# A fused two-block network on one core: modulation loads issued three or four weight blocks behind the place that frees their slots

## The chip, the core and the metric

One core of a Trainium2 chip runs the whole kernel. The time is the device time of one execution in microseconds (us); for the kernel before, three timed runs are given by their median. The profile is one more execution, recorded by the hardware profiler. The engines are TensorE (PE), VectorE (DVE), ScalarE (ACT), GpSimd (POOL) and SyncE (SP), whose queue issues the large DMA loads here.

## The reference, cut to what matters

Two blocks of two layers each work on 256 tokens `x` and 256 context tokens, 1024 wide, in float32. Every layer has six modulation vectors of 1024, computed from a condition vector by a 1024 x 6144 matrix. They scale, shift and gate the normalised tokens around a mixer and a gated feed-forward network of width 2816:

```python
mod = (c_act @ w_mod[l] + b_mod[l])[:, None, :]
modc = cc_act @ w_mod[l] + b_mod[l]
sh1, sc1, g1, sh2, sc2, g2 = jnp.split(mod, 6, axis=-1)
...
x = x + g1 * (y_x @ w_out[l])
x = x + g2 * swiglu(rmsnorm(x, norm2_g[l]) * (1.0 + sc2) + sh2, w_gu[l], w_down[l])
...
def swiglu(h, w_gu, w_down):
    gate, up = jnp.split(h @ w_gu, 2, axis=-1)
    return (jax.nn.silu(gate) * up) @ w_down
```

The second block has the same frame with attention as its mixer and its own matrices `mod_w_2`, `ffn_w_in_2` and `ffn_w_out_2` (in the profile `mod_w`, `ffn_w_in`, `ffn_w_out`). The first two layers are the kernel's layers 0 and 1, the others 2 and 3.

## The kernel before, in words

**Weight blocks.** All large matrices are cut into 210 blocks of 1 MB or less (`Plan.item`, numbered 0 to 209 in the order of use). SP loads them one after another into a ring of four slots (`weight_slots`). The load of block g waits until block g - 4 has been split (`weights`, line 607). Splitting makes two float32r parts of a float32 block: ScalarE writes `weights_high`, and VectorE `weights_low`, the rest. PE multiplies high by high, high by low and low by high, and `weights_high` and `weights_low` hold two blocks each.

**Quarter stages.** In layers 0 and 2 most of the feed-forward's first product runs "by quarters": a block's product is built of seven smaller ones (P1 to P7, each 12 matmuls) on sums of weight quarters and of token halves. GpSimd makes the weight sums (L683 to L691), ScalarE (L2654) and VectorE (L1952) split quarters six steps (`LOOK`) ahead of their multiplication, and VectorE adds the products up (L1982, L1990, L1998). Two blocks, the gate's and the value's side, make a pair. A first run takes pairs 2 to 5 (blocks 20 to 27 in layer 0, 122 to 129 in layer 2), a second run, behind the first half of the down projection, pairs 6 to 10 (blocks 36 to 45 in layer 0). The seven quarters of a block come in the order P7, P6, (P2 of the next block), P5, (P1 of the next block), P3, P4.

**Modulation.** The modulation matrices are used in thirds of a layer's 2048 columns. Eight of the twelve thirds are multiplied on PE, in eight steps each: step s takes 128 rows, a load of 1 MB into one of two `modulation_slots` (slot s % 2, `SIDES` = 2), and eight matmuls. The 64 steps have places in PE's program (`places` in `Plan.schedule`). In the first run of a quarter stage two stand at `("quarters", L)`, behind the first two quarters, and two each at `("hidden", L, 5)`, `("hidden", L, 7)` and `("hidden", L, 9)`, behind the last quarter of pairs 2, 3 and 4. In the second run of layer 0 two each stand behind pairs 7, 8, 9 and 10. Each place is written with a block number g in `places`: the block behind which it stands, for "quarters" the first of the run. The four other thirds are summed on VectorE from small row blocks in the down projections ("blocks" and "conditions" in the load list).

**Order on SP.** SP's program is one list: for each weight block g first the loads that `load_before[g]` names, then block g. A step's load waits, on SP, until PE has multiplied the step that had its slot (`stepped`, two steps earlier). While SP waits, everything behind it in the list waits too. Lines 218 to 225 choose the block before which a step's load stands: six blocks behind the place of step s - 2.

The lines that the change touches are in `Plan.schedule`; the step that uses the result is the loop at the end of `sync_program`. Order is all that follows from `load_before`; the waits of the other engines name events, not positions.

Of the kernel before, what the change touches and what calls it, by code (L numbers as in the profile page):

```python
# [88 lines left out]
SIDES = 2  # L89
# [44 lines left out]
class Plan:  # L134
# [54 lines left out]
    def schedule(self):  # L189

        self.mod_steps, self.mod_turn, self.mod_end = {}, {}, {}
        self.load_before = {}
        places = [(("start", k), -1) for k in range(KD)]
        places += [(("proj", 0, e), self.proj[0][e // 2]) for e in (5, 5, 7, 7, 9, 9, 11, 11)]
        places += [(("mlstm", 0, e), self.proj[0][-1]) for e in range(1, 9)]
        for L, first in ((0, (4, 14)), (2, (4,))):
            if L == 2:
                places += [(("mlstm", 1, e), self.proj[1][-1]) for e in range(1, 9)]
                places += [(("proj", 2, e), self.proj[2][e // 2]) for e in (5, 5, 7, 7, 9, 9, 11, 11)]
            for f0 in first:  # L200
                places += [(("quarters", L), self.gu[L, 2][0])] * 2 if f0 == 4 else []
                places += [(("hidden", L, f | 1), self.gu[L, f // 2][1]) for f in range(f0, f0 + (6 if f0 == 4 else KD))]
        assert len(places) == KD * len(STEPPED)
        self.block_at, u = {}, 0
        for L in FAST:
            for part in range(2):
                for f, n in enumerate(BLOCKS_OF_TILE):
                    self.block_at["down", L, part, f] = range(u, u + n)
                    u += n
        assert u == 16 * len(SUMMED)  # L210
        self.block_of_item = {b: self.down[place[1], place[2]][place[3]] for place, bs in self.block_at.items() for b in bs}
        self.block_after = {0: 4, 16: 5, 32: 8}
        self.step_after = {KD * 4: 15, KD * 5: 31}
        for s, (place, g) in enumerate(places):
            self.mod_steps.setdefault(place, []).append(s)
            if s % KD == KD - 1:
                self.mod_end[place] = s // KD
        for s in range(KD, len(places)):
            n = s - s % KD
            if n in self.step_after and s - n < SIDES:  # L220
                before = self.block_of_item[self.step_after[n]] + 4
            else:
                g = places[s - SIDES][1]
                before = g + 6 if g >= 0 else 3
            self.load_before.setdefault(before, []).append(("step", s))
        for u in range(16 * len(SUMMED)):
            at = u - u % 16
            if at in self.block_after and u - at < 3:
                before = places[KD * self.block_after[at] - 1][1] + 4
                if u == at:  # L230
                    self.load_before.setdefault(before, []).append(("conditions", u // 16))
            else:
                before = self.block_of_item[u - 3] + 4
            self.load_before.setdefault(before, []).append(("block", u))
        self.mod_turn = {("proj", 0, 13): 1, ("mlstm", 0, 9): 2, ("down", 0, 0, 1): 3, ("down", 0, 1, 1): 6, ("mlstm", 1, 9): 7,
                         ("out", 2, 0): 8, ("down", 2, 0, 1): 9}
# [2869 lines left out]
```

## Time and profile before

| | us |
|---|---|
| median of three timed runs | 2156.19 |
| the three runs | 2155.13 to 2156.57 |
| profiled execution | 2149.87 |
| its span, first to last instruction | 2148.4 |
| PE busy | 2033.5 (95%) |
| VectorE busy | 1387.4 (65%) |
| ScalarE busy | 1013.7 (47%) |

Times in the rows are counted from the span's start. In a timeline each row has the start, the time from there to the end of the last of its instructions, the engine, line and operation, and in brackets the idle time before it and what ended that. DMA rows on SP (printed SPq) are issues, not transfers. The first quarter stage of layer 0 lies between 340 and 440 us, its second run between 520 and 637, and the one of layer 2 between 1370 and 1467.

### The profile page before, as it was taken

The numbers are of one execution on the slowest core, as the hardware profiler recorded it, in microseconds if no ns is written. First come the engines' busy times: TensorE is split into PE (matmuls) and PEld (weight loads), VectorE is DVE, ScalarE is ACT, GpSimd is POOL, SyncE is SP. The second block draws the span as 40 slices with busy tenths as digits, with TensorE's granted clock in tenths as the row PEclk, the third lists the DMA queues.
The fourth block names the chain that finished last, engine by engine and source line by source line (L and its number), as shares of the span: only waits on it lengthen the run. The fifth ranks groups of instructions, "written<-read, shape, count | busy, mean of one in ns | idle before, by whom it ended". The sixth has DMA issues, their size and how long they took to land.

```text
span 2148.4 us, 32247 instructions
## 1 busy us (share of the span) xinstructions
PE 2033.5 (95%) x12804; PEld 1683.5 (78%) x12804; DVE 1387.4 (65%) x2299; ACT 1013.7 (47%) x1810; POOL 422.6 (20%) x308
## 2 busy tenths in 40 slices
PE   6999999999999899999999899999999999989999
PEld 4776677888987786999966337788898766769999
DVE  4394657867978666655554434786798865566555
ACT  3444644432543646544553343454255256555443
POOL 1000316512531004100100241552154100000000
PEclk9999999999999999999999999999999999999999
DMA  9641521548448535456535002144832731114564
GB/s 340 210 156 60 177 79 59 187 130 277 139 161 290 177 98 202 148 165 212 158 113 184 18 1 79 59 157 153 274 104 85 225 113 63 59 40 158 164 210 118
DMA packets 276742, 311.62 MB, mean 145 GB/s; under 512 B 6128, under 2 KB 260208, under 8 KB 269424
## 3 DMA queue, kind: packets, MB, share of 16 engines
q1 hardware_dynamic: 271888, 304.90, 43.3%
q10 hardware_dynamic: 4704, 4.65, 0.7%
q8 instruction: 102, 1.67, 0.3%
q14 instruction: 48, 0.39, 0.1%
HBM read 308.48 MB, written 1.05 MB: 144 GB/s over the span
## 4 chain that ended last, share of the span: by engine, by line
PE 69%; DVE 15%; ACT 7%; POOL 3%; DMA 3%; issue 3%; ACTq 0%; SPq 0%; DVEq 0%; POOLq 0%
PE bank L779 68%; DVE weights_low L1571 3%; ACT weights_high L2376 2%; DVE weights_low L1952 2%; DVE scratch L1563 1%; DVE yT L1563 1%; DMA modulation_slots<-p_modulation_rows 1%; DVE input_low L1563 1%; DVE modulation_slots L1597 1%; DMA parameter_columns<-p_columns 1%; PE bank L788 1%; DVE xT L1563 1%; DVE hidden_low L1966 1%; DVE big L2095 1%; DMA modulation_slots<-w_mod 0%
## 5 line engine op out<-in xcount | busy, mean ns | idle before, releaser
L779 PE MATMUL bank<-input_high,weights_high 128*128 128x256 f32 (+1 forms) x2336 | 750.7, 323 | 27.5 <-DVE scratch L1990 10.2
L779 PE MATMUL bank<-input_high,weights_low 128*128 128x256 f32 (+1 forms) x2336 | 736.8, 317 | 0.0
L779 PE MATMUL bank<-input_low,weights_high 128*128 128x256 f32 (+1 forms) x2336 | 715.9, 318 | 5.3 <-DVE input_low L1563 5.2
L779 PEld LDWEIGHTS bank<-input_high,weights_high 128*128 128x128 f32 x2336 | 441.4, 189 | 87.4 <-issue 29.4
L1571 DVE TENSOR_TENSOR weights_low<-weight_slots,weights_high 128x1024 fp32r<-128x1024 f32 (+2 forms) x344 | 386.0, 1161 | 185.3 <-ACT weights_high L2376 185.0
L779 PEld LDWEIGHTS bank<-input_low,weights_high 128*128 128x128 f32 x2336 | 435.1, 189 | 43.2 <-DVE input_low L1563 9.7
L779 PEld LDWEIGHTS bank<-input_high,weights_low 128*128 128x128 f32 x2336 | 441.2, 189 | 33.5
L2376 ACT ACTIVATE weights_high<-weight_slots 128x1024 fp32r<-128x1024 f32 (+2 forms) x348 | 314.4, 950 | 149.5 <-PE bank L779 136.4
L1952 DVE TENSOR_TENSOR weights_low<-weight_slots,weights_high 128x512 fp32r<-128x512 f32 x216 | 233.5, 1100 | 35.3 <-ACT weights_high L2654 33.2
L779 PE MATMUL bank<-hidden_high,weights_high 128*128 128x256 f32 (+1 forms) x704 | 238.5, 339 | 0.6 <-DVE weights_low L1571 0.4
L779 PE MATMUL bank<-hidden_low,weights_high 128*128 128x256 f32 (+1 forms) x704 | 237.4, 337 | 0.0
L779 PE MATMUL bank<-hidden_high,weights_low 128*128 128x256 f32 (+1 forms) x704 | 237.3, 337 | 0.0
L750 POOL TENSOR_TENSOR yT<-yT 128x256 f32<-128x256 f32 (+1 forms) x66 | 67.5, 1027 | 642.7 <-ACT yT L2402 514.4
L2654 ACT ACTIVATE weights_high<-weight_slots 128x512 fp32r<-128x512 f32 x216 | 129.2, 622 | 38.0 <-POOL weight_slots L688 19.7
L779 PEld LDWEIGHTS bank<-hidden_high,weights_high 128*128 128x128 f32 x704 | 132.1, 188 | 18.8 <-issue 2.3
L779 PEld LDWEIGHTS bank<-hidden_high,weights_low 128*128 128x128 f32 x704 | 132.1, 188 | 16.2
L779 PEld LDWEIGHTS bank<-hidden_low,weights_high 128*128 128x128 f32 x704 | 132.2, 188 | 15.7
L1563 DVE SCALAR_TENSOR_TENSOR xT<-bank,modulation,xT 128x256 f32<-128x256 f32 x144 | 64.5, 480 | 123.9 <-PE bank L779 123.1
L779 PE MATMUL bank<-token_sums,weights_high 128*128 128x256 f32 x576 | 105.6, 282 | 4.1 <-ACT scratch L2701 2.6
L683 POOL TENSOR_TENSOR weight_sum<-weight_slots 128x512 f32<-128x512 f32 x36 | 50.5, 1402 | 290.7 <-DVE weights_low L1952 148.5
L2402 ACT ACTIVATE yT<-xT 128x256 f32<-128x256 f32 (+1 forms) x64 | 32.9, 522 | 138.5 <-DVE xT L1563 133.1
L779 PEld LDWEIGHTS bank<-token_sums,weights_high 128*128 128x128 f32 x576 | 88.2, 189 | 5.7 <-ACT scratch L2701 3.4
(284 smaller groups left out, 2773.8 us busy)
## 6 DMA issues: line engine op xcount, KB each, us to landing
weight_slots<-w_gu SPq DMA_DIRECT2D x44, 1024.0 KB, 5.2
weight_slots<-ffn_w_in SPq DMA_DIRECT2D x44, 1024.0 KB, 5.2
modulation_slots<-p_modulation_rows SPq DMA_DIRECT2D x64, 512.0 KB, 4.9
modulation_slots<-mod_w SPq DMA_DIRECT2D x32, 1024.0 KB, 6.6
modulation_slots<-w_mod SPq DMA_DIRECT2D x28, 1024.0 KB, 6.6
weight_slots<-w_in SPq DMA_DIRECT2D x24, 1024.0 KB, 8.1
weight_slots<-w_down SPq DMA_DIRECT2D x16, 768.0 KB, 5.1
weight_slots<-ffn_w_out SPq DMA_DIRECT2D x16, 768.0 KB, 5.1
```

The lines of the kernel that those rows point to most:

```text
L683: pool.tensor_tensor(m.weight_sum[:, :, :], a21, a22, ALU.add).then_inc(m.weights_added.sem, 1)
L750: pool.tensor_tensor(o, yT[:, 2 + q, t] if k == 1 else o, yT[:, 2 + i % 4, t], ALU.add).then_inc(m.square_joined.sem, 1)
L779: return pe.matmul(o, w, r, start=start, stop=stop, skip_group_check=shared)
L788: return pe.transpose(o, a, ident[0:a.shape[0], 0:a.shape[0]])
L1563: return stt(out=o, in0=a, scalar=s, in1=b, op0=op0, op1=op1)
L1571: tt(m.w_low[:, g % 2, c], m.ring[:, g % SLOTS, c], m.w_high[:, g % 2, c].bitcast(F32), ALU.subtract).then_inc(m.low_made.sem, 1)
L1597: stt(out=m.block_slot(u), in0=m.block_slot(u), scalar=1.0, in1=m.condition_row(), op0=ALU.mult, op1=ALU.mult, accum_out=m.mods[:, l4, 0, ...
L1952: tt(low, m.raw(run, j), high.bitcast(F32), ALU.subtract).then_inc(m.low_made.sem, 1)
L1966: tt(m.a_low[:, local, :], m.prod[:, f % 2, :], m.a_high[:, local, :].bitcast(F32), ALU.subtract).then_inc(m.hid_low.sem, 1)
L2376: F(m.w_high[:, g % 2, c], m.ring[:, g % SLOTS, c], ACT.Copy).then_inc(m.high_made.sem, 1)
L2402: F(yT[:, 2 + k % 4, t], xT[:, k, t], ACT.Square).then_inc(m.squared.sem, 1)
L2654: F(m.split(j)[0], m.raw(run, j), ACT.Copy).then_inc(m.high_made.sem, 1)
```

## The change

A step's load is still issued some weight blocks behind the place of step s - 2, but the number depends on the kind of that place: four blocks where it is a "hidden" place, three where it is the "quarters" place, six everywhere else as before.

```diff
             if n in self.step_after and s - n < SIDES:
                 before = self.block_of_item[self.step_after[n]] + 4
             else:
-                g = places[s - SIDES][1]
-                before = g + 6 if g >= 0 else 3
+                place, g = places[s - SIDES]
+                before = g + {"hidden": 4, "quarters": 3}.get(place[0], 6) if g >= 0 else 3
             self.load_before.setdefault(before, []).append(("step", s))
```

Eighteen steps move. The engines' own programs are the same; only SP's list is in another order.

| steps | multiplied at | load before block, before | after |
|---|---|---|---|
| 26, 27 | hidden 5, layer 0 | 26 | 23 |
| 28, 29 | hidden 7 | 27 | 25 |
| 30, 31 | hidden 9 | 29 | 27 |
| 34, 35 | hidden 17 | 45 | 43 |
| 36, 37 | hidden 19 | 47 | 45 |
| 38, 39 | hidden 21 | 49 | 47 |
| 58, 59 | hidden 5, layer 2 | 128 | 125 |
| 60, 61 | hidden 7 | 129 | 127 |
| 62, 63 | hidden 9 | 131 | 129 |

(Steps 32 and 33, the first of a third that waits for summed blocks, keep their place, as do those of the projections.)

SP's list in the first run of layer 0's quarter stage, before. The `w_mod` rows are loads of modulation steps (24 and 25 are the last two of the eight ahead), the `w_gu` rows weight blocks 17 to 25, 26 and 27, and `w_down` block 28:

```order
L595 DMA modulation_slots<-w_mod 128x2048 x8
L611 DMA weight_slots<-w_gu 128x8x256 x9
L595 DMA modulation_slots<-w_mod 128x2048 x2
L611 DMA weight_slots<-w_gu 128x8x256
L595 DMA modulation_slots<-w_mod 128x2048 x2
L611 DMA weight_slots<-w_gu 128x8x256
L611 DMA weight_slots<-w_down 128x12x128
L595 DMA modulation_slots<-w_mod 128x2048 x2
L604 DMA modulation_slots<-p_condition_rows 128x1024
```

The same stretch of SP's list after:

```order
L595 DMA modulation_slots<-w_mod 128x2048 x8
L611 DMA weight_slots<-w_gu 128x8x256 x6
L595 DMA modulation_slots<-w_mod 128x2048 x2
L611 DMA weight_slots<-w_gu 128x8x256 x2
L595 DMA modulation_slots<-w_mod 128x2048 x2
L611 DMA weight_slots<-w_gu 128x8x256 x2
L595 DMA modulation_slots<-w_mod 128x2048 x2
L611 DMA weight_slots<-w_gu 128x8x256
L611 DMA weight_slots<-w_down 128x12x128
L604 DMA modulation_slots<-p_condition_rows 128x1024
```

Steps 26 and 27 now stand ahead of blocks 23, 24 and 25, steps 28 and 29 ahead of blocks 25 and 26, and steps 30 and 31 ahead of block 27. Layer 2 has the same pattern.

SP's list in the second run of layer 0, as a difference; the first row is the load of steps 32 and 33, the `w_gu` rows are blocks 38 to 45 of the run, and the other `mod_w` rows are later steps:

```order
 L595 DMA modulation_slots<-mod_w 128x2048 x2
-L611 DMA weight_slots<-w_gu 128x8x256 x7
+L611 DMA weight_slots<-w_gu 128x8x256 x5
+L595 DMA modulation_slots<-mod_w 128x2048 x2
+L611 DMA weight_slots<-w_gu 128x8x256 x2
 L595 DMA modulation_slots<-mod_w 128x2048 x2
 L611 DMA weight_slots<-w_gu 128x8x256
```

Steps 34 and 35 now stand ahead of blocks 43 and 44, and steps 36 and 37 ahead of block 45.

## Rows read from the trace of the kernel before

**Rows 1.** The page, part 1: busy time, share of the span and instructions of each engine.

```profile
PE 2033.5 (95%) x12804; PEld 1683.5 (78%) x12804; DVE 1387.4 (65%) x2299; ACT 1013.7 (47%) x1810; POOL 422.6 (20%) x308
```

**Rows 2.** Waits of PE over the span: engine, line, waited for, total us, times, longest us.

```profile
PE bank L779 <- DMA modulation_slots<-w_mod: 15.2, 4, 6.7
...
PE bank L779 <- DMA modulation_slots<-mod_w: 3.9, 3, 1.7
```

**Rows 3.** Timeline of PE, layer 0, first run of the quarter stage.

```profile
359.32 1.92 PE L779 MATMUL bank<-modulation_slots,condition_vectors 128*32 128x512 f32 x16
363.73 0.39 PE L779 MATMUL bank<-input_high,weights_high 128*128 128x256 f32 x1 [2.49 <-DVE input_low L1957]
...
385.58 0.28 PE L779 MATMUL bank<-token_sum_high,weights_low 128*128 128x256 f32 x1
389.18 1.07 PE L779 MATMUL bank<-modulation_slots,condition_vectors 128*32 128x512 f32 x8 [3.32 <-DMA modulation_slots<-w_mod]
391.64 1.94 PE L779 MATMUL bank<-modulation_slots,condition_vectors 128*32 128x512 f32 x8 [1.40 <-DMA modulation_slots<-w_mod]
...
415.17 1.92 PE L779 MATMUL bank<-modulation_slots,condition_vectors 128*32 128x512 f32 x16
...
436.98 1.92 PE L779 MATMUL bank<-modulation_slots,condition_vectors 128*32 128x512 f32 x16
```

**Rows 4.** Timeline of PE, layer 2, first run of the quarter stage.

```profile
1416.34 0.28 PE L779 MATMUL bank<-token_sum_high,weights_low 128*128 128x256 f32 x1
...
1418.35 1.07 PE L779 MATMUL bank<-modulation_slots,condition_vectors 128*32 128x512 f32 x8 [1.73 <-DMA modulation_slots<-mod_w]
1420.83 1.60 PE L779 MATMUL bank<-modulation_slots,condition_vectors 128*32 128x512 f32 x8 [1.41 <-DMA modulation_slots<-mod_w]
...
1443.50 1.92 PE L779 MATMUL bank<-modulation_slots,condition_vectors 128*32 128x512 f32 x16
```

**Rows 5.** Timeline of PE, layer 0, second run of the quarter stage.

```profile
548.99 0.28 PE L779 MATMUL bank<-token_sum_high,weights_low 128*128 128x256 f32 x1
...
557.54 0.39 PE L779 MATMUL bank<-input_high,weights_high 128*128 128x256 f32 x1 [1.27 <-DVE scratch L1990]
...
570.68 1.92 PE L779 MATMUL bank<-modulation_slots,condition_vectors 128*32 128x512 f32 x16
```

**Rows 6.** Stretches: us, busy (instructions) by engine, granted clock, DMA share, GB/s.

```profile
363.70:367.00 3.30, 2.80 (x21) 2.60 (x22) 3.30 (x5) 2.23 (x6) 1.90 (x2) 1.00 0.02 5
...
389.00:392.00 3.00, 1.43 (x12) 0.36 (x16) 2.25 (x2) 0.00 (x0) 1.63 (x2) 0.73 0.12 49
392.00:396.50 4.50, 4.50 (x22) 3.00 (x15) 0.00 (x0) 0.03 (x1) 0.00 (x0) 0.50 0.00 0
...
1420.00:1424.00 4.00, 3.17 (x15) 1.80 (x16) 2.01 (x2) 0.00 (x0) 1.46 (x1) 0.65 0.01 4
```

**Rows 7.** Timeline of VectorE, the adds behind the ends of pairs 2 and 6.

```profile
386.15 0.41 DVE L1998 TENSOR_TENSOR scratch<-scratch,bank 128x256 f32<-128x256 f32 x1
...
549.56 0.41 DVE L1998 TENSOR_TENSOR scratch<-scratch,bank 128x256 f32<-128x256 f32 x1
...
557.08 0.41 DVE L1990 TENSOR_TENSOR scratch<-scratch,bank 128x256 f32<-128x256 f32 x1
```

**Rows 8.** Timeline of SP's DMA issues, layer 0, first run of the quarter stage.

```profile
335.42 12.69 SPq L611 DMA_DIRECT2D weight_slots<-w_gu  x2
...
368.90 11.56 SPq L611 DMA_DIRECT2D weight_slots<-w_gu  x2
380.50 1.05 SPq L595 DMA_DIRECT2D modulation_slots<-w_mod  x2
...
438.96 0.33 SPq L604 DMA_DIRECT2D modulation_slots<-p_condition_rows  x1
```

**Rows 9.** Line L595 in 378 to 425 us: issue to landing of its loads.

```profile
DMA to landing us min/median/max: 7.0/8.7/10.5
```

**Rows 10.** Timeline of ScalarE: the splits of two quarters in pair 3.

```profile
409.80 1.15 ACT L2654 ACTIVATE weights_high<-weight_slots 128x512 fp32r<-128x512 f32 x2
```

## The prediction

> **What bounds the kernel now.** I read the page first: TensorE (PE) is busy for 95% of the span [rows 1], so a microsecond in which it stands still counts unless something takes it back later. The second view is the waits of PE. The largest entry there is a DMA: PE waited 15.2 us in four places for a row block of `w_mod` in the modulation slots and 3.9 us in three for one of the second block's matrix (printed `mod_w`) [rows 2]. The third view is PE's timeline through the quarter stages, which says which of these waits the change can reach. In layer 0 the last quarter of pair 2 starts at 385.58 and ends at 385.86; the two steps at `("hidden", 0, 5)` then start at 389.18 and 391.64, after 3.32 and 1.40 us of waiting for their loads [rows 3]. In layer 2 the same place waits 1.73 and 1.41 us [rows 4]. That is 4.72 + 3.14 = 7.86 us. The other 11.2 us of the DMA entry lie in the projections, whose loads the change leaves where they are. The later places of these stages show no wait: the steps at 415.17, 436.98, 570.68 and 1443.50 run straight on [rows 3 to 5].
>
> Why only that place is late is in SP's timeline. The loads of steps 26 and 27 are issued at 380.50 to 381.55 [rows 8]. Their slots came free when steps 24 and 25 were multiplied, and those ended at 359.32 + 1.92 = 361.24 [rows 3]. They stand behind blocks 24 and 25 in SP's program, and block 25 is issued at 368.90 + 11.56 - 0.38 = 380.08 only [rows 8], when block 21 is split. From issue to landing such a load takes 7.0 to 10.5 us [rows 9], and PE gets there 5.4 us after the first issue.
>
> **What the wait costs beside the waiting.** The clean distance from one hidden place to the next is 436.98 - 415.17 = 21.81 us [rows 3]. From the end of the quarters at 385.86 to the next place at 415.17 it is 29.31 us; 29.31 - 21.81 = 7.50 us are lost, 2.78 more than the waiting. In layer 2, 1443.50 - 1416.62 = 26.88 us, so 5.07 us are lost, 1.93 more than the waiting [rows 4]. The rest is TensorE's clock. In 389 to 392 us its granted clock averages 0.73 of full speed, and in 392 to 396.5 it is 0.50, that is 1.2 GHz of 2.4; in layer 2 it averages 0.65 in 1420 to 1424 [rows 6]. Before each fall the engine had waited twice within some 6 us. At the clean places it does the same sixteen modulation matmuls in 1.92 us, and the distances above hold no slow stretch.
>
> The Trainium skill (TensorE: Matmul & The Clock Gate, section "HAM oscillation — how this bites in real kernels") counts this loss as the throttled time times one half. With the shares that the granted clock gives, that is about 1.6 + 4.5 us throttled up to 396.5, so 3.1 us in layer 0 against my 2.8, and 0.35 / 0.5 of 4 us, halved, so 1.4 against 1.9 in layer 2: the sum would move by 0.2 us, and I keep the distances.
>
> **The change part by part.** *Steps 26, 27 and 58, 59 (hidden 5).* They are now issued three blocks behind the place of the quarters, that is before block 23 (125 in layer 2). Their own wait on steps 24 and 25 ends at 361.24; SP goes on within 0.1 us of such an event (438.96 against the end of steps at 438.90) [rows 3, 8]. So they are issued at about 361.3 and 361.9 and have landed by 361.9 + 10.5 = 372.4, 13 us before PE reaches 385.86. Taken: both waits and both slow stretches go, 7.50 + 5.07 = 12.57 us. The bound from below is the waiting alone, 7.86 us, if the clock fell for another reason.
>
> *Block 23 (and 125).* It was issued at 335.42 + 12.69 - 0.37 = 347.74 [rows 8] and now waits for PE's place of the quarters: about 362.4, 15 us later. Its quarters are split six steps ahead of their multiplication, and its first (P2) is multiplied as the third quarter after 385.86. A quarter takes (21.81 - 1.92) / 14 = 1.42 us, so its split would begin near 380. Even after 10.5 us in flight it is there at 373. Cost 0, hidden by seven microseconds.
>
> *Steps 28 to 31 (hidden 7 and 9) and their twins.* They are issued before blocks 25 and 27 instead of 27 and 29. They were not late, so this gains nothing, but it puts the wait for PE ahead of those blocks. In the new program steps 26 and 27 end at 385.86 + 1.92 = 387.8. Step 28 goes out at 386.9, step 29 at 387.9, block 25 at about 388.4 instead of 380.08. Behind SP stand only more loads. Who waits for block 25 is ScalarE, whose L2654 splits its P2, then GpSimd's weight sums. ScalarE splits the corresponding pair of quarters at 409.80, 5.4 us before the clean place at 415.17 [rows 10]; the clean place of the new program is at 385.86 + 21.81 = 407.7, so block 25 is wanted near 402.3. It lands at 388.4 + 10.5 = 398.9 at the latest by [rows 9]. Cost 0, with 3.4 us in hand. The same distance holds for blocks 27, 43, 45, 127 and 129. Block 47 is a `w_down` block that is multiplied only after the last quarter.
>
> *The summed blocks.* The condition row and modulation blocks ahead of block 29 keep their place and wait for the last step at hidden 9 as before (438.96) [rows 8]. PE, VectorE, ScalarE and GpSimd keep their programs.
>
> *Sum.* -12.57 us and no added term. The profiled execution took 2149.87 us, so its like should take 2137.3. The median of the timed runs is 2156.19, 6.3 us above the profiled one for a reason that the profile can't show; I take the same difference from it: 2156.19 - 12.57 = 2143.6 us, 0.58% less.
>
> **Rivals.** *A, VectorE takes some of it back.* VectorE uses the stall to catch up, and without it PE could wait for its adds instead, as it does at 557.54 for 1.27 us behind L1990, one pair end earlier where no modulation step stands [rows 5]. There L1990 starts 557.08 - 549.56 = 7.52 us after L1998 [rows 7]. At the place in question L1998 starts at 386.15 [rows 7], so L1990 would be done at 386.15 + 7.52 + 0.41 = 394.1. There PE had ended the pair before at 548.99 + 0.28 = 549.27 and began to wait at 557.54 - 1.27 = 556.27, 7.0 us later [rows 5]. At the place in question it wants the same add 7.0 us after it resumes, at 387.8 + 7.0 = 394.8, since the steps themselves give VectorE 1.9 us. That speaks against it, by 0.7 us. If it came nonetheless, 1.27 us in each layer: 2143.6 + 2.5 = 2146.1 us.
>
> *B, only the waiting comes back.* If the clock stays low for a while anyway, or timed runs didn't pay for it, the gain is 7.86 us: 2156.19 - 7.86 = 2148.3 us. For it speaks that waits of only 1.73 and 1.41 us were followed by a fall in layer 2; against it, that the wait of 2.49 us before 363.73 [rows 3] left the clock at 1.00 [rows 6]. The Trainium skill (TensorE: Matmul & The Clock Gate, section "Part 1: The HAM clock gate") says that the number of slow matmuls differs between runs of one kernel.
>
> *C, the stall moves.* The loads no longer come late but something else ends as late, a transfer or a split that stood in the stall's shadow, and the time stays at 2156. Against it stands the clean pair that follows: from 415.17 to 436.98 the same instructions run without a wait [rows 3].
>
> *D, slower: the blocks behind SP's wait come late.* Six blocks (25, 27, 43, 45, 127, 129) now start only after a hidden place. If one lands over 3.4 us later than the 10.5 us I allow, ScalarE waits for it in order and its copies out of PSUM behind it, so PE soon waits too. It decides the sign when the six lose over 12.5 us, 2.1 us each, that is landings 16 us after issue: 2156.2 + 6 at, say, 3.1 us each = 2162 us. Against it: the longest landing in this stretch was 10.5 us, with three megabytes queued at once, just as it will be now [rows 9]. The Trainium skill (DMA: Bandwidth & Descriptors, section "Queues, rings and completion order") says that descriptors of one queue are consumed in ring order on each DMA engine, which would make the block, now third of three, land last: at the 10.5 us and not at the 5 to 7 us of a block that goes first.
>
> **How the numbers follow.** The forecast 2143.6 has a chance of 0.66, A 0.12, B 0.10, C 0.07, D 0.05. A measurement of this kernel can tell about 0.2% (4.3 us) from no change. The forecast, A and B are all faster by more: 0.88; C is within it: 0.07; D slower: 0.05. The range takes in the forecast, A and B: its upper end is B's 2148.3 with 1.2 us for the spread of medians. Its lower end, 2140.0, allows for timed runs whose loads landed later than in the profile, so that more stall was there to remove (the spread of three runs is 1.4 us, and 6.3 us of them are unexplained).
>
> **What would show it.** Right: no wait of PE for the modulation slots near 386 and 1416; hidden 5 to hidden 7 in 21.8 us in both layers, granted clock 1.00 there; SP issuing steps 26 and 27 near 361 and block 25 near 388; PE's wait for `w_mod` down from 15.2 to 10.5 us and for `mod_w` from 3.9 to 0.8 us. A: a wait behind L1990 near 395. B: a granted clock under 1 there without a DMA wait. D: waits of ScalarE at L2654 or of GpSimd at L683 for `weight_slots` loads around 402, 587 and 1433. The prediction is wrong if anything in PE's program before 359 us moves, since nothing there is touched.

## The result and the profile after

The changed kernel takes 2142.55 us in the median of six runs (2135.34 to 2146.80) and the kernel before, run beside it, 2155.66 us (six runs, 2149.89 to 2156.57). The ratio is 0.9945 with a 95% interval from 0.9929 to 0.9961: 0.55% less, where 0.58% was forecast. In a later comparison on one chip the same pair gave 2139.00 and 2151.40 us, again 0.9945 (0.9926 to 0.9963).

The profiled execution of the changed kernel, however, took 2146.80 us (span 2145.3), only 3.1 us less than that of the kernel before (2149.87, span 2148.4). So the first question is whether the two stretches lost what was forecast, and the second what took 9.5 us back in this execution. Here are the first four waits of PE over the whole span (total us, times, longest):

```profile
PE bank L779 <- DMA modulation_slots<-w_mod: 10.6, 2, 6.9
PE bank L779 <- DVE scratch L1990: 9.3, 10, 1.3
PE bank L779 <- DVE modulation_slots L2235: 8.6, 3, 4.1
PE bank L779 <- DVE weights_low L1571: 7.2, 7, 4.4
```

The entry for `w_mod` fell from 15.2 us in four places [rows 2] to 10.6 us in two, both in the first 13 us of the program, and the one for `mod_w` from 3.9 us in three places to 1.0 us in one, at a step that the change does not move. PE's timeline at the places of [rows 3] in layer 0:

```profile
363.36 1.92 PE L779 MATMUL bank<-modulation_slots,condition_vectors 128*32 128x512 f32 x16
367.75 0.39 PE L779 MATMUL bank<-input_high,weights_high 128*128 128x256 f32 x1 [2.46 <-DVE input_low L1957]
...
389.79 1.92 PE L779 MATMUL bank<-modulation_slots,condition_vectors 128*32 128x512 f32 x16
...
411.60 1.93 PE L779 MATMUL bank<-modulation_slots,condition_vectors 128*32 128x512 f32 x16
```

and at those of [rows 4] in layer 2:

```profile
1418.47 1.92 PE L779 MATMUL bank<-modulation_slots,condition_vectors 128*32 128x512 f32 x16
...
1440.29 1.92 PE L779 MATMUL bank<-modulation_slots,condition_vectors 128*32 128x512 f32 x16
```

From hidden 5 to hidden 7 it is now 411.60 - 389.79 = 21.81 us and 1440.29 - 1418.47 = 21.82 us, where 29.31 and 26.88 us had passed [rows 3, 4]. The steps at hidden 5 start right when the quarters end. That is 7.50 + 5.06 = 12.56 us less. SP's issues in the same stretch (compare [rows 8]):

```profile
364.49 1.20 SPq L595 DMA_DIRECT2D modulation_slots<-w_mod  x2
365.73 7.56 SPq L611 DMA_DIRECT2D weight_slots<-w_gu  x2
390.92 1.20 SPq L595 DMA_DIRECT2D modulation_slots<-w_mod  x2
392.16 4.19 SPq L611 DMA_DIRECT2D weight_slots<-w_gu  x2
```

Steps 26 and 27 go out 1.1 us after the quarters place has started, and block 25 at 392.16, held until hidden 5. It landed 9.2 us later, at 401.4, and ScalarE split its first quarters at 406.29. The loads of the steps in this stretch (line L595, 360 to 420 us) now took 4.8 to 8.3 us to land, against 7.0 to 10.5 [rows 9]. ScalarE's waits in this profile name no load of `w_gu` or `ffn_w_in`.

What took 9.5 us back is TensorE's clock in places that the change doesn't touch. The stretch from 200 to 230 us is the entry of layer 0's mLSTM mixer. The columns are those of [rows 6]; first the kernel before, then the changed one, then the second profile of the changed one:

```profile
200.00:230.00 30.00, 25.56 (x152) 15.87 (x152) 18.65 (x54) 19.31 (x34) 13.47 (x18) 1.00 0.24 78
```

```profile
200.00:230.00 30.00, 26.14 (x118) 16.46 (x119) 14.83 (x42) 16.55 (x27) 10.04 (x14) 0.77 0.13 40
```

```profile
200.00:230.00 30.00, 25.56 (x152) 15.90 (x152) 18.66 (x54) 19.31 (x34) 13.51 (x18) 1.00 0.25 78
```

PE got through 152 matmuls in 30 us where the granted clock was 1.00, and through 118 where it averaged 0.77. The changed kernel did one in its first profile and the other in its second. Another fall of this kind came at 820 us in the first profile. The second one, with neither, has a span of 2130.5 us, 17.9 us under the kernel before's: 12.6 us of the change and some luck with the clock. The mean granted clock of the three spans says the same: 0.990 before, 0.986 and 0.994 in the two profiles of the changed kernel. Taken times the span, the missing share is 21.5, 30.0 and 12.8 us: in the first profile it rose by 8.5 us although the two stretches had stopped falling. Between the two executions of one program it differs by 17.2 us, and their spans by 14.8.

### The profile page after: what moved, and what is told of

It reads as the page before. It is cut to its first block, busy times and chain, and to the rows that moved or that the text cites. A ratio compares the mean times of both kernels' runs of the same rounds, so it can differ in the third digit from the quotient of the medians.

```text
span 2145.3 us, 32247 instructions
## 1 busy us (share of the span) xinstructions
PE 2040.3 (95%) x12804; PEld 1689.0 (79%) x12804; DVE 1384.9 (65%) x2299; ACT 1014.1 (47%) x1810; POOL 423.0 (20%) x308
## 4 chain that ended last, share of the span: by engine, by line
PE 71%; DVE 14%; ACT 7%; POOL 3%; issue 3%; DMA 2%; ACTq 0%; DVEq 0%; POOLq 0%
PE bank L779 70%; DVE weights_low L1571 3%; ACT weights_high L2376 1%; DVE weights_low L1952 1%; DVE scratch L1563 1%; DVE yT L1563 1%; DMA modulation_slots<-p_modulation_rows 1%; DVE input_low L1563 1%; DVE modulation_slots L1597 1%; PE bank L788 1%; DMA parameter_columns<-p_columns 1%; DVE xT L1563 1%; DVE hidden_low L1966 1%; DVE big L2095 1%; ACT big L2901 0%
## 5 line engine op out<-in xcount | busy, mean ns | idle before, releaser
L779 PE MATMUL bank<-input_high,weights_high 128*128 128x256 f32 (+1 forms) x2336 | 750.3, 323 | 26.6 <-DVE scratch L1990 9.3
```

The lines of the kernel that those rows point to most:

```text
L779: return pe.matmul(o, w, r, start=start, stop=stop, skip_group_check=shared)
```

## The experiments

**Only the number for the quarters place.** Three blocks behind the quarters place, six behind the hidden ones.

```diff
-                before = g + {"hidden": 4, "quarters": 3}.get(place[0], 6) if g >= 0 else 3
+                before = g + {"quarters": 3}.get(place[0], 6) if g >= 0 else 3
```

> Only the number for the quarters place is changed: steps 26, 27 and 58, 59 are issued before blocks 23 and 125, all other steps six blocks behind as in the kernel before. Theory (only the loads for hidden 5 were late): the whole gain, 12.6 us in the two stretches (hidden 5 to hidden 7 in 21.8 us in layers 0 and 2, no wait of PE for the modulation slots there), so the same time as the changed kernel within 0.2%. Rival (the earlier loads at hidden 7 and 9 bring a part): more than 21.8 us between hidden 7 and hidden 9 or a new wait for the slots at hidden 7, and a time over the changed kernel's by more than 4 us.

Measured: 2140.01 us against 2150.33 for the kernel before on the same chip, 0.9948 (0.9932 to 0.9964), the changed kernel's own ratio within 0.03%.

```profile
389.56 1.93 PE L779 MATMUL bank<-modulation_slots,condition_vectors 128*32 128x512 f32 x16
...
411.38 1.92 PE L779 MATMUL bank<-modulation_slots,condition_vectors 128*32 128x512 f32 x16
...
433.20 1.92 PE L779 MATMUL bank<-modulation_slots,condition_vectors 128*32 128x512 f32 x16
```

That is PE's timeline at hidden 5, 7 and 9: 21.82 us between each, and no wait. In layer 2 it is 1438.26 - 1416.43 = 21.83 us. The fourteen loads that the other number moves bring nothing that these runs can see. The whole gain in the two stretches is in steps 26, 27, 58 and 59. The medians differ by 10.3 us (7.7 to 14.6 by the interval), which holds the 12.6 us.

**The smallest move.** The same, but only one block earlier than before.

```diff
-                before = g + {"hidden": 4, "quarters": 3}.get(place[0], 6) if g >= 0 else 3
+                before = g + {"quarters": 5}.get(place[0], 6) if g >= 0 else 3
```

> The smallest move that should do: steps 26, 27 and 58, 59 are issued before blocks 25 and 127, one block earlier than in the kernel before (block 26), and nothing else moves. Theory (they were late because SP held them behind block 25 until 380): they go out behind block 24 near 369.3, land by 380 (7.0 to 10.5 us after issue), 6 us ahead of PE, and the gain is again 12.6 us. Rival (their transfer itself is slow at this time, or they need the 25 us of the full move): a wait of PE at hidden 5 of 1 us or more remains.

Measured: 2142.58 us against 2150.33, 0.9961 (0.9949 to 0.9974). The issues of SP there, and what PE then does at hidden 5 and 7:

```profile
371.94 0.37 SPq L611 DMA_DIRECT2D weight_slots<-w_gu  x1
372.35 1.05 SPq L595 DMA_DIRECT2D modulation_slots<-w_mod  x2
383.15 0.38 SPq L611 DMA_DIRECT2D weight_slots<-w_gu  x1
```

```profile
388.84 1.92 PE L779 MATMUL bank<-modulation_slots,condition_vectors 128*32 128x512 f32 x16
...
410.67 1.92 PE L779 MATMUL bank<-modulation_slots,condition_vectors 128*32 128x512 f32 x16
```

The loads go out at 372.35, 16 us ahead of PE, and the wait is gone, with 21.83 us to the next place in both layers (1412.86 to 1434.69 in layer 2). So the cause was the one named: the loads stood behind block 25, which SP could not issue before block 21 was split. The timed gain is smaller than the stretches say: 7.8 us, 5.6 to 11.0 by the interval, which leaves out 12.6. Its ratio lies 0.13% above the first experiment's and the two intervals overlap, so these five runs don't show that one block is worth less than three; what the missing microseconds are stays open.

**One block too early at the hidden places.** The changed kernel with a three instead of the four.

```diff
-                before = g + {"hidden": 4, "quarters": 3}.get(place[0], 6) if g >= 0 else 3
+                before = g + {"hidden": 3, "quarters": 3}.get(place[0], 6) if g >= 0 else 3
```

> The changed kernel with three blocks instead of four behind a hidden place: steps 28, 29 are now issued before block 24, so block 24 (and 26, 42, 44, 126, 128) waits for hidden 5 and is issued near 388.4 although its first quarter is wanted for splitting near 392. It lands at 394 to 399, 2 to 7 us late. Theory of rival D (a late block stops ScalarE in order, and PE behind it): a wait of ScalarE at L2654 for a weight_slots load at six places, PE loses 1 to 6 us at each, 6 to 30 us slower than the changed kernel. The other view (the splits run six quarters, 8.5 us, ahead, and that absorbs it): within 4 us of the changed kernel.

Measured: 2168.14 us against 2150.33, 1.0084 (1.0069 to 1.0098): slower than the kernel before by 17.8 us, and by 28.1 us than the first experiment's kernel, which ran beside it and differs from this one by the hidden places' number alone. This is ScalarE's timeline behind hidden 5, and PE's:

```profile
389.87 0.63 ACT L2654 ACTIVATE weights_high<-weight_slots 128x512 fp32r<-128x512 f32 x1
394.85 0.63 ACT L2654 ACTIVATE weights_high<-weight_slots 128x512 fp32r<-128x512 f32 x1 [4.35 <-DMA weight_slots<-w_gu]
```

```profile
383.23 1.92 PE L779 MATMUL bank<-modulation_slots,condition_vectors 128*32 128x512 f32 x16
...
400.38 0.50 PE L779 MATMUL bank<-token_sums,weights_high 128*128 128x256 f32 x2 [0.72 <-ACT scratch L2701]
405.41 0.39 PE L779 MATMUL bank<-input_high,weights_high 128*128 128x256 f32 x1 [1.96 <-DVE scratch L1990]
408.44 1.92 PE L779 MATMUL bank<-modulation_slots,condition_vectors 128*32 128x512 f32 x16
```

Block 24 was issued only behind hidden 5, at 385.6, and ScalarE waited 4.35 us for it. The pair took 408.44 - 383.23 = 25.21 us. The six pairs behind a hidden place took 25.21, 26.43, 27.55, 26.89, 26.29 and 25.19 us, 26.6 us more than six times 21.82. ScalarE's waits for blocks sum to 29.2 us in six places. Behind hidden 5 the granted clock was 1.00 (385 to 409 us), so that pair's loss is waiting and not the clock; in the second run it averaged 0.94 (568 to 624 us), so a part of the loss there is the clock. So a block that comes late costs PE nearly its whole lateness, although the splits run six quarters ahead: ScalarE works in order, and its copies out of PSUM stand behind the split that waits. PE's waits name ScalarE and VectorE, never the load. The lookahead view has fallen; rival D's mechanism is real, one block further on.

**Filling the wait, first try.** The kernel before, with throwaway matmuls in front of the two late steps (`keep_busy` multiplies a 128x128 tile into bank 4, which nothing uses there).

```diff
+        fill = {("hidden", 0, 5): (26, 10), ("hidden", 2, 5): (13, 10)}.get(place, (0, 0))
         for s in m.mod_steps.get(place, ()):
+            keep_busy(4, fill[s % 2])
             mod_step(s)
```

> The kernel before with its loads as late as they were, but PE multiplies throwaway 128x128 tiles in front of each of the two steps at hidden 5: 26 and 10 in layer 0, 13 and 10 in layer 2, at 0.12 us each, that is 3.1, 1.2, 1.6 and 1.2 us of the 3.3, 1.4, 1.7 and 1.4 us that it waited. Theory (12.6 us are 7.9 us of waiting and 4.7 us of the clock that fell behind it): granted clock 1.00 from 389 to 402 and from 1420 to 1428, hidden 5 to hidden 7 in 26.5 us in layer 0 (385.9 to 412.4) and 25.0 us in layer 2, 4.7 us less in sum, so 0.2% faster than the kernel before. Rival (the slow stretch comes from the waiting PE's queue or from the transfers, not from an engine that did nothing): the distances stay at 29.3 and 26.9 us.

Measured: 2151.95 us against 2150.33, 1.0006 (0.9994 to 1.0019). The clock part came as expected, the distances did not, since the fill was too long. PE's timeline and one stretch of it:

```profile
385.48 5.97 PE L779 MATMUL bank<-ident,mean_over_d 128*128 128x128 f32 x52
391.37 1.06 PE L779 MATMUL bank<-modulation_slots,condition_vectors 128*32 128x512 f32 x8
392.37 2.50 PE L779 MATMUL bank<-ident,mean_over_d 128*128 128x128 f32 x20
```

```profile
389.00:402.00 13.00, 13.00 (x110) 11.08 (x110) 4.75 (x7) 3.47 (x8) 1.50 (x1) 1.00 0.14 45
```

Each float32 throwaway is two rows of the trace, so 26 of them took 5.97 us and not 3.1. From the end of the quarters to hidden 7 it was 30.2 us in layer 0 and 27.7 in layer 2. The granted clock stayed at 1.00 where it had been 0.73 and 0.50 [rows 6], and also from 1413 to 1428 us in layer 2.

**Filling the wait, sized.** 15 and 6 in layer 0, 7 and 6 in layer 2.

```diff
+        fill = {("hidden", 0, 5): (15, 6), ("hidden", 2, 5): (7, 6)}.get(place, (0, 0))
```

> The kernel before with throwaway matmuls ahead of the steps at hidden 5 again, now sized by what one took in the run before (0.215 us and not 0.12): 15 and 6 in layer 0, 7 and 6 in layer 2, that is 3.2, 1.3, 1.5 and 1.3 us of waiting that they fill. Theory (the rest of the loss is the clock): granted clock 1.00 in both stretches, from the end of the quarters to hidden 7 26.5 us in layer 0 and 25.0 us in layer 2, 4.7 us less than in the kernel before. Rival (the loss has another source): 29.3 and 26.9 us although the clock stays at 1.00.

Measured: 2146.47 us against 2151.40, 0.9984 (0.9969 to 0.9999). PE's timeline in layer 0:

```profile
384.74 0.28 PE L779 MATMUL bank<-token_sum_high,weights_low 128*128 128x256 f32 x1
384.86 3.51 PE L779 MATMUL bank<-ident,mean_over_d 128*128 128x128 f32 x30
388.30 1.06 PE L779 MATMUL bank<-modulation_slots,condition_vectors 128*32 128x512 f32 x8
389.29 1.60 PE L779 MATMUL bank<-ident,mean_over_d 128*128 128x128 f32 x12
390.83 1.07 PE L779 MATMUL bank<-modulation_slots,condition_vectors 128*32 128x512 f32 x8
...
411.85 1.92 PE L779 MATMUL bank<-modulation_slots,condition_vectors 128*32 128x512 f32 x16
```

From 385.02 to 411.85 it is 26.8 us, against 29.3 before and 26.5 expected; in layer 2 it was 25.4 against 26.9 and 25.0. The loads are as late as in the kernel before (issued 5.4 us ahead of the end of the quarters in both layers), yet 4.0 us of the two stretches are gone, with the granted clock at 1.00 from 385 to 412 and from 1410 to 1440 us. That splits the 12.57 us: about a third was the clock that fell behind PE's standing still, the rest the standing still. The timed difference is 4.9 us, but its interval is wide, 0.2 to 6.7 us, and the distances come from one profile of each kernel; the first try's profile also stayed at 1.00 in both stretches.

**The changed kernel again.** The same program.

> The changed kernel once more, beside the next two on the same chip, since its profiled span (2145.3) was only 3.1 us under the one of before although the two stretches had lost 12.6 us. Theory (the other 9.5 us are TensorE's clock, which falls in other places in some executions and not in others): the two distances are 21.8 us again, the granted clock is under 1 in other places than in the first profile, and the median is 10 to 14 us under the kernel before. Rival (the change itself costs 9 us somewhere): the same places between 200 and 360 us and behind 567 us are slow again, and the median is only 3 to 5 us better.

Measured: 2139.00 us against 2151.40, 0.9945 (0.9926 to 0.9963). The distances are 405.08 - 383.26 = 21.82 us and 1427.29 - 1405.47 = 21.82 us. The slow stretches of the first profile at 200 to 230 and at 820 us are not there, as the third row of stretches above shows. The rival that the change itself costs 9 us has fallen.

**Filling the entry of the mLSTM mixers.** The changed kernel with throwaway matmuls at two waits of PE.

```diff
                 if h > 1:
+                    if h == 2 and s == 0:
+                        keep_busy(4, 8)
                     pe.wait_ge(*out_.at(L, h - 2))
...
+            if which:
+                keep_busy(4, 6)
             for j in range(2):
                 pe.wait_ge(*m.ln_s.at(L, 6 * which + j))
```

> The changed kernel with throwaway matmuls where PE waits at the entry of the mLSTM mixers in layers 0 and 1: 6 ahead of the second layer norm's variance (1.3 us of a wait of 1.4) and 8 ahead of the third head's key transposes (1.7 us of a wait of 1.75). There the clock fell in the changed kernel's profile (210 to 225 us, 820 to 830 us) and not in the kernel before's, with the same waits. Theory (the fall follows from PE's short idle stretches, and whether it comes differs between executions): no fall there, up to 7 and 5 us less in executions that had one, a median 2 to 6 us under the changed kernel's. Rival (the clock falls for another reason, or the fill costs what it saves): the same median or up to 2 us more.

Measured: 2137.88 us against 2151.40, 0.9940 (0.9924 to 0.9955). The stretch:

```profile
200.00:230.00 30.00, 28.65 (x182) 19.14 (x181) 18.97 (x57) 19.32 (x34) 14.44 (x18) 1.00 0.28 90
```

The clock stayed at 1.00 there. But in the same profile it fell a little later:

```profile
250.00:260.00 10.00, 8.49 (x34) 7.67 (x35) 4.09 (x11) 8.05 (x30) 1.30 (x1) 0.66 0.62 214
```

Over the whole set of profiles of kernels without this fill (before, changed twice, and the five other experiments) it fell in that stretch in three of eight, and averaged 0.77 there each time. Five of eight stayed at 1.00 without any fill, so one profile at 1.00 doesn't show that the fill did it, and the theory of this experiment stays unproven. The runs of this version lie between 2135.24 and 2139.89 us, the changed kernel's beside it between 2132.00 and 2144.87. That is a narrower spread, but the medians differ by 1.1 us only, and five runs against six don't settle whether this version is faster. It is the fastest median of this study, unproven.

## Why the prediction was right, and where not

**The place and the size of the stall** were right to a tenth: 7.50 and 5.07 us forecast, 7.50 and 5.06 measured, with the clean distance of the neighbouring pairs as the yardstick. Taking the distance from place to place, and not the waits, brought in the third that the waits don't show. The sized fill shows this part by itself, at 4.0 us against the 4.7 us of the sum, so it was over-estimated by at most 0.7 us. Rival B, that only the 7.86 us of waiting come back, is out by the clean distances; the timed gains of the changed kernel, 13.1 and 12.4 us, have intervals from 8.4 and 8.0 us up, only just above it. One argument against B was weaker than it looked: the wait of 2.49 us that left the clock at 1.00 did not always leave it there (see the last section).

**The cause** (SP held the loads behind block 25) was right; one block earlier is enough to end the wait. Two readings beside it were off and cost nothing. The other 11.2 us of PE's waits for these loads are not in the projections: 10.5 lie in the first 13 us of the program and 0.8 at 853 us, and none of these loads moves. And step 26 went out 1.1 us after the quarters place began, not about 2, since it waits for step 24 alone.

**Edits costed at nothing.** Steps 28 to 31 and their twins cost nothing and bring nothing. I had block 25 at 2.5 us after the start of the hidden place and it went out 392.16 - 389.79 = 2.4 us after. It landed 9.2 us later (10.5 allowed) and was used 16.5 us after the start of the place, as forecast, so 4.9 us were in hand where I had 3.4. That this slack decides the sign is shown by the hidden-3 kernel. My price for a late block, lateness nearly one to one on PE, also held roughly: 26.6 us of PE, a part of it clock, for 29.2 us of ScalarE's waiting.

**Rival A** did not come: PE has no wait at all from 385 to 420 and from 1415 to 1463 us, as the 0.7 us of margin said. Rival C is refuted by the clean distances.

**What failed** is the step from one profiled execution to another. I wrote that the like of the profiled run should take 2137.3 us, and that the prediction is wrong if anything before 359 us moves. It took 2146.8, and the quarters place moved from 359.32 to 363.36 with no instruction changed there. In the second profile of the same program it stood at 356.79. The term that I had missed is the clock outside the two stretches. It makes most of the ten microseconds and more by which executions of one program differ. The same thing probably explains the 6.3 us between median and profile that I could not account for, though no clock of those three timed runs is on record: the kernel before's own seventeen runs beside the last experiments span 2145.40 to 2156.01 us, and their mean granted clock goes from 0.992 in the fastest to 0.984 to 0.987 in the six slowest. The median was forecast well because the stall is in the median of the kernel before and not in that of the changed one, while the clock's falls elsewhere are in both. That the absolute 2143.6 us was met within 1.1 us is partly luck: it rests on carrying over the unexplained 6.3 us, and in the later comparison both kernels were lower by about as much. There the kernel before took 2151.40 us, 4.8 under the base of the forecast, and the changed one 2139.00 us, 4.6 under the forecast and just under the range's lower end of 2140.0. The difference held better than the time.

## What to carry to other kernels

A load that waits for nothing itself can be late because the queue's program has it behind one that does; compare the issue time with the time its slot came free. When such a load is moved ahead, its own wait goes ahead of the blocks behind it, and how far is read from when the next engine wants those blocks: one block further turned 0.55% faster into 0.84% slower. Size a stall on PE by the distance to the next like place against a clean one, since a third of it can lie behind the wait, in the clock.

## What the runs showed of the hardware

TensorE's granted clock can fall to half behind short pauses. In layer 2 of the kernel before it fell behind two waits of 1.73 and 1.41 us [rows 4, 6]. With throwaway matmuls in these pauses and the loads as late as before, it stayed at 1.00.

One pause can come before a fall too. Behind the quarters place PE has one wait of 2.45 to 2.50 us in all nine profiles. In six of them, the kernel before's among them [rows 3, 6], the clock stayed at 1.00 behind it, and in three it fell. This is the changed kernel's first profile, behind the wait that ended at 367.75:

```profile
367.70:371.00 3.30, 3.25 (x17) 3.26 (x18) 3.30 (x5) 2.13 (x6) 1.88 (x2) 0.57 0.99 420
```

That fall cost nothing: from the quarters place to hidden 5 it was 26.43 us with it, and 26.47 us in the second profile, without it. So a low clock is not by itself a loss; the distance to the next place says whether it is one.

Whether it falls behind pauses of the same length is not fixed. The entry of the mLSTM mixer has the same waits in the kernel before and the changed one, 1.4, 1.7 and 0.4 us:

```profile
PE bank L788 <- DVE big L1842: 1.7, 1, 1.7
PE bank L779 <- ACT big L2490: 1.4, 1, 1.4
```

These two rows are from the changed kernel's waits of PE in 195 to 222 us, where the clock fell, and they read the same in the kernel before and in the changed kernel's second profile, where it did not. What decides it is not settled by these runs. The Trainium skill (TensorE: Matmul & The Clock Gate, section "Part 1: The HAM clock gate") says, of the start of a kernel, that the number of slow matmuls varies from run to run. Here the falls in mid-kernel vary too: the changed kernel's two profiles averaged 0.77 and 1.00 between 200 and 230 us.
